# Two-layer attention and RWKV trunk: the next round's key norm begun in the levels, gates in the last round's levels, half the attention out projection in its chunk steps

## The chip, the cores and the metric

The kernel runs on one core of a Trainium2 chip. The metric is device time in microseconds (us), the median of its runs. PE is the matrix engine, DVE the vector engine, ACT the scalar (activation) engine, POOL the GpSimd engine, SP the engine that issues most DMAs; each runs its own instructions in the order in which they are written, and semaphores order the engines among one another.

## The reference

Two layers over 256 tokens of width 1024, float32. One layer, cut to what matters here:

```python
p = x @ w_in                                  # q, k, v, indexer; two gates; r, k, v, lora inputs of the RWKV part
y_a = dsa_sparse_mqa(...)                     # 8 heads over the top 64 keys that an indexer picks, then @ w_oa
kk = hd(k * k_k)
kk = kk / jnp.maximum(jnp.linalg.norm(kk, axis=-1, keepdims=True), 1e-12)      # the key norm
k = k * (1 + (a - 1) * k_a)
def step(state, inp):                         # 16 heads of 64, over 256 tokens
    sa = jnp.einsum('bhvk,bhk->bhv', state, -kk_t)
    state = state * w_t + sa[..., None] * b_t + v_t[..., None] * k_t
    return state, jnp.einsum('bhvk,bhk->bhv', state, r_t)
y_b = (group_norm(y) + bonus) * g @ w_ob
g_a, g_b = jnp.split(jax.nn.sigmoid(p_gate + b_gate), 2, axis=-1)
x = layer_norm(alpha * x + (g_a * y_a + g_b * y_b) @ w_out)
x = layer_norm(alpha * x + conv_glu_ffn(x))
```

## The kernel before

**A layer.** It runs through these stages: a prologue (projections, the indexer's scores), four rounds g = 0 to 3, the attention out projection ("oa", four pairs of weight slots), the RWKV one ("ob", four pairs), the mix ("out") and the feed-forward network ("up", "down"). Weights come through a ring of four slots that SP fills in the order of stream_order.

**A round.** It handles 4 of the 16 heads. The recurrence is done in 4 chunks of 64 tokens. PE first makes the grams (L836 and L877, which read arc, the scaled kk and r, and b_k, the scaled b and k) and turns v, b and k to token rows (V, tokB, tokK). Then come six levels of a doubling inverse on 64x64 blocks: per level W (copied out by ACT, L1246), X and Y (copied by DVE with a mask, L1572, and transposed, L1577), and W^T Y at the last. Then four chunk steps Z, Q, S, y, each a matmul, an ACT or DVE step, and the next matmul. All this is small and serial, so PE is given other products in between: fill(n) is called at 14 gaps of the levels and 8 of the chunk steps, and runs what the tables put there. A *piece* is half of one weight slot's product: 12 matmuls of 128x256 (three rounded parts per product, L700 to L702) inside the rounds; ahead of the first round the pieces are plain float32 (L679), two to a slot.

**What the tables put where.** LEVEL_GAPS puts the 8 pieces of the next round's r and k projections (pairs "rkv") into the levels, chunk_pairs its v projection and one gate (two in the last round) into the chunk steps. The last round has nothing in its levels. Five further gaps hold fixed work: the attention's logits, y_back (the last round's y turned back), the bonus, the probabilities' transposes (L818) and the values (L828 to L830). A slot's weights are split on ACT and DVE: "mid" (cast L1143, remainder L1462, two buffers) for pieces in rounds, "split" (cast L1178, remainder L1697, four buffers) for whole pairs after them.

**The preparation of a round.** It makes arc and b_k from the r and k projections. In the rounds before it: prep_kk on ACT (squares of the scaled key, L1190) after att_o; prep_1 on PE (decay and a lora products, L743 and L746) after the levels; then ACT's tanh (L1197), DVE's prep_decay (L1490 to L1494) and ACT's exponentials; prep_2 (in layer 1 the value lora's product; the key's sums of squares "ss", L764, 8 matmuls) after chunk 0, prep_3 (rnT, L769) after chunk 1, prep_4 (rnx, L778) after chunk 2; DVE's prep_sum, prep_rn and prep_rest (kkn L1533 to b_k L1551) in chunk steps 1 to 3. At a layer's start the same parts stand between the pieces of the first three gates, and DVE's two top-k searches (L1867 to L1880) stand between prep_sum, prep_rn and prep_rest. The grams wait for b_k and, after a round, for the sum of its y (y_sum, L1632).

**After the rounds.** PE does pairs oa 0 and 1, y_back, oa 2 and 3, ob 0 to 3. DVE centres, scales and gates y (L1632 to L1657), the halves yb 0 and yb 1 are rounded for ob, and gated_o (L1946) takes an oa pair's sum out of PSUM.

## Time and profile before

| what | value |
|---|---|
| runs | 1255.3, 1255.31, 1260.0 us |
| median | 1255.31 us |
| the profiled execution: its own time | 1254.65 us |
| its span, first to last instruction | 1252.4 us |
| mean granted PE clock | 0.977 |
| PE busy | 1152.6 us (92%) |
| DVE busy | 785.4 us (63%) |
| ACT busy | 539.0 us (43%) |
| POOL busy | 54.5 us (4%) |

Times in the rows below are us from the start of the span. A granted clock of 1.00 is 2.4 GHz, 0.50 is 1.2 GHz. Busy says how long an engine had an instruction in it, the brackets of a timeline row how long it stood idle before it and what released it.

### The profile page before, as it was taken

To read this page: it belongs to the slowest core of one execution; us is meant where nothing else is said; L and a number is where in the kernel's file an instruction comes from. 1 tells how busy PE (TensorE), PEld (TensorE's weight loads), DVE (VectorE), ACT (ScalarE), POOL (GpSimd) and SP (SyncE) were. 2 spreads that over 40 slices of the span, in tenths; PEclk is the share of its full clock that TensorE was granted. 3 is DMA by queue.
4 is the path that set the end of the run, shared out by engine and by line. 5 is a ranking of instruction groups with operands and counts; after the bars stand their busy time and mean duration, and the time that the engine had idled before them with its cause. 6 is when DMAs were issued, how large, how long until landed. Compare 5 with 4: busy or idle time off the path is not lost.

```text
span 1252.4 us, 29267 instructions
## 1 busy us (share of the span) xinstructions
PE 1152.6 (92%) x12328; PEld 1038.1 (83%) x12328; DVE 785.4 (63%) x1436; ACT 539.0 (43%) x938; POOL 54.5 (4%) x56
## 2 busy tenths in 40 slices
PE   7997998997899899999899979989978998999997
PEld 7777887876789799998797768878767897999985
DVE  1267576667476777774512775757584767777745
ACT  2243535353354355553212445353534443555531
POOL 0000000000000100000100000000000001000000
PEclk9999999999999899999999999999999998999998
DMA  7422221211175456556454221212111754555561
GB/s 283 147 90 77 85 91 50 83 52 61 35 260 178 162 178 195 182 195 200 152 179 147 77 73 69 94 53 87 42 53 38 265 170 168 179 192 178 193 200 69
DMA packets 45353, 165.38 MB, mean 132 GB/s; under 512 B 5136, under 2 KB 5392, under 8 KB 44976
## 3 DMA queue, kind: packets, MB, share of 16 engines
q1 hardware_dynamic: 42576, 154.02, 36.6%
q0 software_dynamic: 1504, 7.47, 1.8%
q8 instruction: 98, 1.61, 0.5%
q10 hardware_dynamic: 1152, 2.10, 0.5%
q14 instruction: 23, 0.19, 0.0%
HBM read 160.42 MB, written 3.15 MB: 131 GB/s over the span
## 4 chain that ended last, share of the span: by engine, by line
PE 76%; DVE 16%; issue 3%; ACT 3%; DMA 1%; DVEq 0%; SPq 0%; ACTq 0%
PE ps L700 18%; PE ps L701 16%; PE ps L702 16%; PE ps L836 8%; PE ps L679 5%; PE ps L986 3%; DVE ring_r L1462 2%; PE ps L848 1%; DVE keep L1873 1%; PE ps L1028 1%; DVE small L1871 1%; DMA ring<-stream_dram 1%; DVE X_Y L1577 1%; DVE X_Y L1572 1%; DVE keep L1860 1%
## 5 line engine op out<-in xcount | busy, mean ns | idle before, releaser
L700 PE MATMUL ps<-x_tok_r,mid_hi 128*128 128x256 f32 x448 | 137.7, 307 | 13.7 <-DVE ring_r L1462 12.5
L701 PE MATMUL ps<-xT_r,mid_hi 128*128 128x256 f32 x448 | 127.1, 284 | 0.0
L702 PE MATMUL ps<-x_tok_r,ring_r 128*128 128x256 f32 x448 | 126.9, 283 | 0.0
L700 PEld LDWEIGHTS ps<-x_tok_r,mid_hi 128*128 128x128 f32 x448 | 85.8, 191 | 23.4 <-issue 15.6
L679 PE MATMUL ps<-xT,ring 128*128 128x256 f32 x448 | 99.7, 381 | 0.0
L679 PEld LDWEIGHTS ps<-xT,ring 128*128 128x128 f32 x448 | 84.2, 190 | 13.0 <-issue 1.6
L701 PEld LDWEIGHTS ps<-xT_r,mid_hi 128*128 128x128 f32 x448 | 86.1, 192 | 0.0
L702 PEld LDWEIGHTS ps<-x_tok_r,ring_r 128*128 128x128 f32 x448 | 86.0, 192 | 0.0
L1572 DVE COPY_PREDICATED X_Y<-masks,ps 128x256 f32<-128x256 uint32 x80 | 35.1, 439 | 63.1 <-PE ps L836 55.3
L1462 DVE TENSOR_TENSOR ring_r<-ring,mid_hi 128x1024 fp32r<-128x1024 f32 x56 | 68.0, 1218 | 5.2 <-ACT mid_hi L1143 4.7
L1697 DVE TENSOR_TENSOR w_lo<-ring,w_hi 128x1024 fp32r<-128x1024 f32 x44 | 53.9, 1225 | 26.6 <-ACT w_hi L1178 26.5
L1697 DVE TENSOR_TENSOR rs_ks_r<-ring,tha_kkn_r 128x1024 fp32r<-128x1024 f32 x46 | 56.3, 1225 | 21.4 <-ACT tha_kkn_r L1178 21.4
L1697 DVE TENSOR_TENSOR vs_dC_r<-ring,b_k_r 128x1024 fp32r<-128x1024 f32 x46 | 56.1, 1220 | 17.4 <-ACT b_k_r L1178 17.4
L1697 DVE TENSOR_TENSOR X_Y_r<-ring,arc_r 128x1024 fp32r<-128x1024 f32 x44 | 53.7, 1222 | 21.1 <-ACT arc_r L1178 21.1
L1178 ACT CAST tha_kkn_r<-ring 128x1024 fp32r<-128x1024 f32 x46 | 47.9, 1041 | 33.7 <-PE ps L702 33.7
L1143 ACT CAST mid_hi<-ring 128x1024 fp32r<-128x1024 f32 x56 | 58.7, 1052 | 8.2 <-PE ps L702 8.2
L836 PE MATMUL ps<-X_Y,nT_rb 64*64 64x64 f32 x1280 | 54.2, 225 | 8.2 <-DVE ak_rk L1564 3.1
L1246 ACT COPY W_bt<-ps 128x256 f32<-128x256 f32 x80 | 29.5, 372 | 71.3 <-PE ps L836 51.1
L701 PE MATMUL ps<-oT_r,tha_kkn_r 128*128 128x256 f32 x208 | 59.8, 288 | 0.0
L836 PEld LDWEIGHTS ps<-X_Y,nT_rb 64*64 64x64 f32 x1280 | 44.6, 137 | 17.0 <-DVE X_Y L1572 7.4
L701 PE MATMUL ps<-oT_r,w_hi 128*128 128x256 f32 x208 | 58.4, 281 | 0.0
L701 PE MATMUL ps<-oT_r,arc_r 128*128 128x256 f32 x208 | 58.4, 281 | 0.0
(435 smaller groups left out, 3385.1 us busy)
## 6 DMA issues: line engine op xcount, KB each, us to landing
ring<-stream_dram SPq DMA_DIRECT2D x281, 512.0 KB, 3.5
lora_w<-lora_dram POOLq DMA_DIRECT2D x2, 1536.0 KB, 7.4
W_bt<-rpar_dram POOLq DMA_DIRECT2D x4, 512.0 KB, 5.2
kt_V<-rpar_dram POOLq DMA_DIRECT2D x4, 512.0 KB, 6.0
x_tok<-x_dram SPq DMA_DIRECT2D x2, 512.0 KB, 4.1
v_saved_dram<-vs_dC ACTq DMA_DIRECT2D x4, 256.0 KB, 4.0
x_tok<-x_dram SPq DMA_DIRECT2D x1, 1024.0 KB, 4.8
vf<-v_saved_dram ACTq DMA_DIRECT2D x4, 256.0 KB, 3.9
```

The costliest lines, as they stand in the source:

```text
L679: mm = pe.matmul(dst[:, b, :], w[:, kb * P:kb * P + P], rhs[:, kb, :], start=(kb == 0), stop=(kb == KB - 1))
L700: pe.matmul(dst, lh, rh, start=start, stop=False)
L701: pe.matmul(dst, lh, rl, start=False, stop=False)
L702: return pe.matmul(dst, ll, rh, start=False, stop=stop)
L836: mm = pe.matmul(dst[q], left[q, u, :], right[q], start=start, stop=stop)
L986: mm = pe.matmul(dst, xT[:, kb, t * P:t * P + P], w[:, kb * P:kb * P + n], start=(kb == 0), stop=(kb == KB - 1))
L1143: act.copy(mid_hi[m % NM][:, :], ring[:, n % RING, :]).then_inc(*act_mid.inc(l, m))
L1178: act.copy(w_hi[m % NS], ring[:, n % RING, :]).then_inc(*act_split.inc(l, m))
L1246: act.copy(W[:, 4 * k:4 * k + 4, :], half64("W", k)).then_inc(*act_wkv.inc(r, f"W{lev}{k}"))
L1462: dve.tensor_tensor(rounded["ring"][:, k, :], ring[:, k, :], f32(mid_hi[m % NM][:, :]), ALU.subtract).then_inc(*dve_mid.inc(l, m))
L1572: dve.copy_predicated(dst[:, 4 * k:4 * k + 4, :], mask_of(which, lev, 4), half64("XW", k)).then_inc(*dve_wkv.inc(r, name))
L1697: dve.tensor_tensor(w_lo[m % NS], ring[:, n % RING, :], f32(w_hi[m % NS]), ALU.subtract).then_inc(*dve_split.inc(l, m))
```

## The change

In words, by place:

- **Levels, g = 1 to 3:** LEVEL_GAPS becomes gaps 0, 1 and 4 to 9 (it was 0 to 7). tokK, which stood alone between gaps 1 and 2, is interleaved with W of level 1; its akV, rkV and ktV move half a level on each.
- **The last round:** its two gates (8 pieces) go into the levels, the pairs oa 0 and 1 (8 pieces, now "mid") into the chunk steps. After the rounds stand oa 2 and 3 alone, y_back after three of their four blocks; ob starts on yb 0 and waits for yb 1 at its seventh block of rows.
- **The next round's preparation:** ss moves from chunk 0 to gap 13 of the levels, rnT from chunk 1 to chunk 0, rnx from chunk 2 to chunk 1; prep_kk on ACT from after att_o to ahead of att_pT in level 4. DVE's prep_rest is cut into keys (c = 1), arc (c = 2) and v, b, k (c = 3).
- **A layer's start:** the parts between the pieces are now (ss), (lora products), (value lora), (rnT); rnx comes after the eighth piece; DVE takes ss first, ahead of prep_decay.

```diff
-LEVEL_GAPS = [list(range(4, 12))] + [list(range(8))] * (GROUPS - 2)
+LEVEL_GAPS = [list(range(4, 12))] + [[0, 1] + list(range(4, 10))] * (GROUPS - 1)
+OA_EARLY = 2
...
 def chunk_pairs(g):
 
+    if g + 1 == GROUPS:
+        return [("oa", i) for i in range(OA_EARLY)]
+    return [("rkv", 3 * (g + 1) + 2)] + gates_of(g)
+
+
+def gates_of(g):
+
     start = GATES_FIRST + sum(GATES_CHUNKS[:g])
-    v = [("rkv", 3 * (g + 1) + 2)] if g + 1 < GROUPS else []
-    return v + [("gate", i) for i in range(start, start + GATES_CHUNKS[g])]
+    return [("gate", i) for i in range(start, start + GATES_CHUNKS[g])]
+
+
+def level_pairs(g):
+
+    return [("rkv", 3 * (g + 1)), ("rkv", 3 * (g + 1) + 1)] if g + 1 < GROUPS else gates_of(g)
...
+            def prep_ss(r):
+
+                l, g = divmod(r, GROUPS)
+                if g == 0:
+                    pe.wait_ge(*act_att(l, "qT"))
+                else:
+                    pe.wait_ge(*act_wkv(r - 1, "ktV"))
                 pe.wait_ge(*act_prep(r, "kk2"))
                 for b in range(GB):
                     for t in range(TT):
                         j = 2 * (TT * b + t)
-                        mm = pe.matmul(bank(7)[:, j:j + 2], tmp[:, b, t * P:t * P + P], C["hsel"], start=True, stop=True)
+                        mm = pe.matmul(bank(4)[:, j:j + 2], tmp[:, b, t * P:t * P + P], C["hsel"], start=True, stop=True)
                 mm.then_inc(*pe_prep.inc(r, "ss"))
 
-            def prep_3(r):
+            def prep_rnT(r):
...
                         w = per_head(half64("W", k)[:, u - 4 * k, :], nT, X[:, u, :], u)
                         if u == 4 * k + 3:
                             w.then_inc(*pe_wkv.inc(r, f"W1{k}"))
-                        side = swapped(unit64(5)[:, u, :], ak[:, u, :], Vc[:, u, :])
+                        if u == 0:
+                            pe.wait_ge(*dve_wkv(r, "akrk"))
+                        side = turned_unit(unit64(5), k_of, u, OTHER)
                     if k == 0:
                         fill(4)
...
+                    if g + 1 < GROUPS and c == 1:
+                        prep_rnx(r + 1)
                     if c:
                         pe.wait_ge(*dve_wkv(r, f"Z{c}"))
                     for b, u in enumerate(bc(c)):
                         mm = per_head(step64(3)[:, b, :], Y, Zs[:, b, :] if c else akV[:, u, :], u)
                     mm.then_inc(*pe_wkv.inc(r, f"Q{c}"))
                     fill(15 + 2 * c)
+                    if g + 1 < GROUPS and c == 0:
+                        prep_v(r + 1)
+                        prep_rnT(r + 1)
...
                 first = sum([pair_pieces(l, ("gate", i), xT) for i in range(GATES_FIRST)], [])
-                for k, p in enumerate((prep_1, prep_2, prep_3, prep_4)):
+                for k, p in enumerate((prep_ss, prep_1, prep_v, prep_rnT)):
                     p(r0)
                     for piece in first[2 * k:2 * k + 2]:
                         piece()
+                prep_rnx(r0)
                 for piece in first[8:]:
                     piece()
...
-                        more = pair_pieces(l, ("rkv", 3 * (g + 1)), xT) + pair_pieces(l, ("rkv", 3 * (g + 1) + 1), xT)
-                        for n, p in enumerate(more):
-                            gaps[LEVEL_GAPS[g][n]].append(p)
+                    for n, p in enumerate(sum([pair_pieces(l, p, xT) for p in level_pairs(g)], [])):
+                        gaps[LEVEL_GAPS[g][n]].append(p)
...
+                    if g + 1 < GROUPS:
+                        gaps[VALUES].append(lambda: prep_ss(r0 + g + 1))
...
-                pe.wait_ge(*dve_parts(l, "o1"))
-                split_pair(l, ("oa", 0), lambda kb: (block_of(o_hi, kb), rounded["oT"][:, kb, :]))
-                split_pair(l, ("oa", 1), lambda kb: (block_of(o_hi, kb), rounded["oT"][:, kb, :]))
+                oa = [b for i in range(OA_EARLY, 4) for b in split_blocks(l, ("oa", i), o_parts)]
+                for block in oa[:-1]:
+                    block()
                 y_back(r0 + GROUPS - 1)
-                for i in (2, 3):
-                    split_pair(l, ("oa", i), lambda kb: (block_of(o_hi, kb), rounded["oT"][:, kb, :]))
-                pe.wait_ge(*dve_parts(l, "yb1"))
+                oa[-1]()
+
+                def yb_parts(kb):
+                    if kb in (0, 6):
+                        pe.wait_ge(*dve_parts(l, f"yb{kb // 6}"))
+                    return block_of(yb_hi, kb), rounded["yb"][:, kb, :]
+
                 for i in range(4):
-                    split_pair(l, ("ob", i), lambda kb: (block_of(yb_hi, kb), rounded["yb"][:, kb, :]))
+                    for block in split_blocks(l, ("ob", i), yb_parts):
+                        block()
 
...
                         for t in range(2):
-                            if nxt and level_before(g, t) == lev:
-                                rkv(l, g + 1, t)
+                            if level_before(g, t) == lev:
+                                if nxt:
+                                    rkv(l, g + 1, t)
+                                else:
+                                    gate(l, gates_of(g)[t][1])
                         if lev == 4:
+                            if nxt:
+                                prep_kk(r + 1)
                             att_pT(l, g)
+                        if not nxt and lev == 4:
+                            act.copy(o_hi[0], blocks(oT, 0, 4)).then_inc(*act_parts.inc(l, "o0"))
                     att_o(l, g)
+                    if not nxt:
+                        act.wait_ge(*act_att(l, f"o{g}"))
+                        act.copy(o_hi[1], blocks(oT, 4, 4)).then_inc(*act_parts.inc(l, "o1"))
...
+
+                prep_ss(r0)
                 prep_decay(r0)
-                prep_sum(r0)
+                prep_pend(r0)
                 topk(0)
                 prep_rn(r0)
                 topk(1)
-                prep_rest(r0)
+                prep_keys(r0)
+                prep_arc(r0)
+                prep_v(r0)
+                prep_bk(r0)
                 prep_bonus(r0)
...
                                 rkv(l, g + 1, t)
                         if lev == 3:
                             att_norm(l, g)
+                        if not nxt and lev == 4:
+                            o_low(0)
                     if nxt:
...
                         prep_decay(r + 1)
+                    if not nxt:
+                        o_low(1)
...
-                                                  f32(o_hi[c - 2]), ALU.subtract).then_inc(*dve_parts.inc(l, f"o{c - 2}"))
+                            if nxt and c == 1:
+                                prep_keys(r + 1)
+                            elif nxt and c == 2:
+                                prep_arc(r + 1)
+                            elif nxt:
+                                prep_v(r + 1)
+                                prep_bk(r + 1)
                         if c < NCH - 1:
                             chunk_s(r, c)
+                        if nxt and c == 0:
+                            prep_pend(r + 1)
+                            prep_rn(r + 1)
```

PE at the first layer's start. The rows follow the indexer's last score; lora,lora_w are the lora products of prep_1, const,tmp is ss (two units in a row), xT,ring the float32 pieces of gate 0. Of before:

```order
L743 MATMUL ps<-lora,lora_w 128x256 [waits act_att,lora_landed,act_lora]
L746 MATMUL ps<-lora,lora_w 128x256
L743 MATMUL ps<-lora,lora_w 128x256
L746 MATMUL ps<-lora,lora_w 128x256
L679 MATMUL ps<-xT,ring 128x256 [waits slot0_landed,dve_dense]
L679 MATMUL ps<-xT,ring 128x256 x3
L679 MATMUL ps<-xT,ring 128x256 [waits slot0_landed]
L679 MATMUL ps<-xT,ring 128x256 x3
L764 MATMUL ps<-const,tmp 128x2 [waits act_prep]
L764 MATMUL ps<-const,tmp 128x2 x3
```

Of the change:

```order
L798 MATMUL ps<-const,tmp 128x2 [waits act_prep,act_att]
L798 MATMUL ps<-const,tmp 128x2 x3
L697 MATMUL ps<-xT,ring 128x256 [waits slot0_landed,dve_dense]
L697 MATMUL ps<-xT,ring 128x256 x3
L697 MATMUL ps<-xT,ring 128x256 [waits slot0_landed]
L697 MATMUL ps<-xT,ring 128x256 x3
L770 MATMUL ps<-lora,lora_w 128x256 [waits act_att,lora_landed,act_lora]
L773 MATMUL ps<-lora,lora_w 128x256
L770 MATMUL ps<-lora,lora_w 128x256
L773 MATMUL ps<-lora,lora_w 128x256
```

The sums of squares stand ahead of the lora products, and a whole slot of gate 0 (16 matmuls) stands between the two.

ACT in levels 4 and 5 of the first round. rs_ks<-ps takes out the next round's k projection, scratch<-ps is att_pT, W_bt<-ps the copies of W for level 5, mid_hi the cast of a weight slot, oT the values, tmp<-rs_ks prep_kk. Of before:

```order
L1132 ACTIVATE rs_ks<-ps,dpar 128x256 [waits slot_used]
L1132 ACTIVATE rs_ks<-ps,dpar 128x256
L1237 COPY scratch<-ps 128x768 [waits pe_att]
L1246 COPY W_bt<-ps 128x256 [waits pe_wkv]
L1143 CAST mid_hi1<-ring 128x1024 [waits slot_used,slot3_landed]
L1246 COPY W_bt<-ps 128x256 [waits pe_wkv]
L1241 COPY oT<-ps 128x512 [waits pe_att]
L1190 ACTIVATE tmp<-rs_ks,cpar 128x256 [waits pe_bonus,dve_dense]
L1190 ACTIVATE tmp<-rs_ks,cpar 128x256
```

Of the change:

```order
L1181 ACTIVATE rs_ks<-ps,dpar 128x256 [waits slot_used]
L1181 ACTIVATE rs_ks<-ps,dpar 128x256
L1239 ACTIVATE tmp<-rs_ks,cpar 128x256 [waits pe_bonus,dve_dense]
L1239 ACTIVATE tmp<-rs_ks,cpar 128x256
L1286 COPY scratch<-ps 128x768 [waits pe_att]
L1295 COPY W_bt<-ps 128x256 [waits pe_wkv]
L1192 CAST mid_hi1<-ring 128x1024 [waits slot_used,slot3_landed]
L1295 COPY W_bt<-ps 128x256 [waits pe_wkv]
L1290 COPY oT<-ps 128x512 [waits pe_att]
```

prep_kk has moved ahead of att_pT and of both copies of W, and it waits for DVE's side of the k projection (dve_dense).

DVE at the end of the last round. b_k and ring_r are splits of weights (here named by the buffers they share), gates<-gates is gated_o, yt<-ps the sum of y, g8, yt and yb its norm. Of the change:

```order
L1673 TENSOR_TENSOR Zs<-ps,sq 128x128 [waits pe_wkv]
L1758 TENSOR_TENSOR w_lo2<-ring,w_hi2 128x1024 [waits act_split]
L1693 TENSOR_TENSOR yt<-ps,yt 128x512 [waits pe_wkv,act_wkv]
L1953 SCALAR_TENSOR_TENSOR gates<-gates,ps 128x512 [waits act_dense,slot_used]
L1697 TENSOR_REDUCE g8<-yt 128x8 [waits dve_y]
L1699 TENSOR_SCALAR g8<-g8 128x8 [waits dve_y]
L1701 TENSOR_TENSOR yt<-yt,g8 128x512 [waits dve_y]
L1758 TENSOR_TENSOR X_Y_r<-ring,arc0_r 128x1024 [waits act_split]
L1706 TENSOR_REDUCE g8<-sq 128x8 [waits act_y]
L1710 TENSOR_TENSOR yt<-yt,g8 128x512 [waits pool_y]
L2027 TENSOR_TENSOR yb_r<-yb,yb_hi0 128x1024 [waits act_parts]
L2027 TENSOR_TENSOR yb_r<-yb,yb_hi1 128x512
```

Of before, from the sum of y on (L1697 is a split there, and L1636 the reduction that is L1697 above):

```order
L1632 TENSOR_TENSOR yt<-ps,yt 128x512 [waits pe_wkv,act_wkv]
L1636 TENSOR_REDUCE g8<-yt 128x8 [waits dve_y]
L1638 TENSOR_SCALAR g8<-g8 128x8 [waits dve_y]
L1640 TENSOR_TENSOR yt<-yt,g8 128x512 [waits dve_y]
L1645 TENSOR_REDUCE g8<-sq 128x8 [waits act_y]
L1697 TENSOR_TENSOR X_Y_r<-ring,arc0_r 128x1024 [waits act_split]
L1649 TENSOR_TENSOR yt<-yt,g8 128x512 [waits pool_y]
L1697 TENSOR_TENSOR rs_ks_r<-ring,tha_kkn_r 128x1024 [waits act_split]
L1946 SCALAR_TENSOR_TENSOR gates<-gates,ps 128x512 [waits act_dense,slot_used]
```

The sum of y and the norm behind it stand among fewer splits, and with one gated_o ahead of the centring.

## Rows read from the trace of the kernel before

**Rows 1.** The page, part 4: the chain that ended last, share of the span by engine.

```profile
PE 76%; DVE 16%; issue 3%; ACT 3%; DMA 1%; DVEq 0%; SPq 0%; ACTq 0%
```

**Rows 2.** Waits of PE, whole span: line, tile, releaser, us in total, times, longest us.

```profile
PE ps L836 <- DVE yt L1632: 15.0, 6, 2.5
...
PE ps L818 <- DVE scratch L1686: 6.2, 6, 1.0
PE ps L836 <- DVE b_k L1551: 6.1, 2, 4.1
```

**Rows 3.** Windows: stretch, us; busy us and instructions of each engine; granted clock, DMA.

```profile
296.94:329.07 32.13, 25.84 (x632) 22.17 (x633) 20.63 (x42) 11.78 (x30) 1.83 (x2) 0.89 0.04 13
329.07:351.43 22.36, 18.92 (x232) 16.73 (x233) 9.64 (x17) 8.06 (x14) 0.00 (x0) 1.00 0.22 72
351.43:363.10 11.67, 11.67 (x102) 11.53 (x100) 8.53 (x11) 7.27 (x9) 2.94 (x4) 1.00 0.91 337
168.81:206.50 37.69, 34.85 (x729) 31.28 (x729) 26.72 (x50) 17.06 (x39) 2.80 (x2) 1.00 0.21 68
```

**Rows 4.** Windows of round starts and of one idle stretch, columns as in rows 3.

```profile
168.81:171.65 2.84, 2.83 (x128) 2.77 (x128) 1.45 (x4) 0.00 (x0) 0.00 (x0) 1.00 0.34 128
232.05:236.61 4.56, 4.56 (x129) 4.49 (x129) 1.61 (x4) 0.00 (x0) 0.00 (x0) 0.63 0.19 74
421.40:427.00 5.60, 1.51 (x10) 0.85 (x8) 4.94 (x8) 2.29 (x3) 1.56 (x1) 0.98 0.00 0
426.80:433.60 6.80, 6.05 (x27) 5.68 (x28) 6.80 (x10) 3.86 (x5) 1.10 (x2) 0.50 0.52 207
```

**Rows 5.** Timeline, first layer's start: start, us, engine, line, op, tiles, count.

```profile
77.88 0.90 ACT L1190 ACTIVATE tmp<-rs_ks,cpar 128x256 f32<-128x256 f32 x2
...
78.27 3.72 PE L679 MATMUL ps<-xT,ring 128*128 128x256 f32 x16
78.68 0.82 ACT L1197 ACTIVATE dA<-ps,dpar 128x256 f32<-128x256 f32 x2
...
81.83 0.95 PE L764 MATMUL ps<-const,tmp 128*128 128x2 f32 x8
...
82.90 0.28 DVE L1867 TENSOR_TENSOR keep<-keep,const 128x128 f32<-128x128 f32 x1
```

**Rows 6.** Timeline, level 4 of the first round: ACT and DVE.

```profile
138.87 0.80 ACT L1237 COPY scratch<-ps 128x768 f32<-128x768 f32 x1
...
139.88 0.37 ACT L1246 COPY W_bt<-ps 128x256 f32<-128x256 f32 x1 [0.21 <-PE ps L836]
...
140.26 0.83 DVE L1453 SCALAR_TENSOR_TENSOR rs_ks<-ps,cpar,rs_ks 128x255 f32<-128x255 f32 x2
...
143.12 0.91 ACT L1190 ACTIVATE tmp<-rs_ks,cpar 128x256 f32<-128x256 f32 x2
```

**Rows 7.** Timeline, end of the second round, start of the third: DVE, then PE.

```profile
230.09 1.22 DVE L1462 TENSOR_TENSOR ring_r<-ring,mid_hi 128x1024 fp32r<-128x1024 f32 x1
...
231.22 0.68 DVE L1632 TENSOR_TENSOR yt<-ps,yt 128x512 f32<-128x512 f32 x1
...
232.05 0.33 PE L836 MATMUL ps<-arc,b_k 64*64 64x128 f32 x2 [2.50 <-DVE yt L1632]
```

**Rows 8.** Waits of PE in the last round of the first layer.

```profile
PE ps L848 <- DVE yt L1649: 1.9, 1, 1.9
PE ps L700 <- DVE ring_r L1462: 1.5, 2, 0.8
PE ps L836 <- DVE S L1625: 1.2, 3, 0.6
...
PE ps L836 <- DVE Zs L1612: 0.8, 1, 0.8
```

**Rows 9.** Timeline after the last round: DVE's sum of y, PE's first ob product.

```profile
353.88 0.68 DVE L1632 TENSOR_TENSOR yt<-ps,yt 128x512 f32<-128x512 f32 x1
...
370.87 0.39 PE L700 MATMUL ps<-o_hi,w_hi 128*128 128x256 f32 x1 [0.84 <-DVE gates L1946]
```

More of the change, by code:

```diff
@@ L100, in mid_gaps @@
     for g in range(GROUPS):
-        if g + 1 < GROUPS:
-            last += [GAPS * g + n for n in LEVEL_GAPS[g][1::2]]
+        last += [GAPS * g + n for n in LEVEL_GAPS[g][1::2]]
         last += [GAPS * g + 14 + chunk_gap(g, 2 * i + 1) for i in range(2 * len(chunk_pairs(g)))]
@@ L151 @@
 SPLIT = ("oa", "ob", "out", "up", "down")
-SPLITS = [s for s in SLOTS if s[1] in SPLIT]
+SPLITS = [s for s in SLOTS if s[1] in SPLIT and not (s[1] == "oa" and s[2] < 2 * OA_EARLY)]
 SPLIT_AT = {s: m for m, s in enumerate(SPLITS)}
 NS = 4
-MIDS = [s for s in SLOTS if s[1] == "gate" and s[2] >= 2 * GATES_FIRST or s[1] == "rkv" and s[2] % KB >= GB]
+MIDS = [s for s in SLOTS if s[1] == "gate" and s[2] >= 2 * GATES_FIRST or s[1] == "rkv" and s[2] % KB >= GB
+        or s[1] == "oa" and s[2] < 2 * OA_EARLY]
 MID_AT = {s: m for m, s in enumerate(MIDS)}
@@ L489, in trunk @@
         pool_att = by_layer("pool_att", ["eps", "rs"])
-        pe_prep = Steps(sem("pe_prep"), [["zw", "za"] + (["zv"] if r >= GROUPS else []) + ["ss", "rnT", "rnx"]
+        pe_prep = Steps(sem("pe_prep"), [["ss", "zw", "za"] + (["zv"] if r >= GROUPS else []) + ["rnT", "rnx"]
                                          for r in range(R)])
@@ L804, in att_logits @@
                 r = GROUPS * l + g
[L805 removed]
+                pe.wait_ge(*act_wkv(r, "tokB"))
                 for h in range(2):
@@ L1248, in levels @@
                 if lev == 1:
+                    act.wait_ge(*pe_wkv(r, "tokK"))
+                    act.copy(kt, unit64(5)).then_inc(*act_wkv.inc(r, "tokK"))
                     act.wait_ge(*pe_wkv(r, "akV"))
@@ L1392, in _ @@
                                 gate(l, i)
-                            else:
+                            elif kind == "rkv":
                                 rkv(l, g + 1, 2)
                         if c == 1 and nxt and l:
-                            prep_tanh(r + 1, "thv", "hv0", kkn, 6)
-                        if not nxt and c in (1, 2):
-                            act.wait_ge(*act_att(l, f"o{g}"))
-                            act.copy(o_hi[c - 1], blocks(oT, 4 * (c - 1), 4)).then_inc(*act_parts.inc(l, f"o{c - 1}"))
+                            prep_tanh(r + 1, "thv", "hv0", thv, 6)
                         if not nxt and c >= 2:
@@ L1881, in topk, with o_low, gated_o @@
                                       ).then_inc(*dve_att.inc(l, f"keep{t}"))
+                def o_low(i):
+                    dve.wait_ge(*act_parts(l, f"o{i}"))
+                    dve.tensor_tensor(blocks(rounded["oT"], 4 * i, 4), blocks(oT, 4 * i, 4), f32(o_hi[i]), ALU.subtract
+                                      ).then_inc(*dve_parts.inc(l, f"o{i}"))
+                def gated_o(i):
+                    dve.wait_ge(*pair_done(l, ("oa", i)))
+                    dve.wait_ge(*act_dense(l, ("gate", 7)))
+                    dst = flat2(gates[:, 2 * i:2 * i + 2, :])
+                    dve.scalar_tensor_tensor(out=dst, in0=dst, scalar=1.0, in1=bank(pair_at[l, ("oa", i)] % 2), op0=ALU.add,
+                                             op1=ALU.mult).then_inc(*dve_dense.inc(l, ("oa", i)))
+                prep_ss(r0)
                 prep_decay(r0)
-                prep_sum(r0)
+                prep_pend(r0)
                 topk(0)
```

171 lines of the change are left out of this document (87 added, 84 removed).

## Prediction, made before the changed kernel ran

> **What bounds the kernel now.** I read the chain that ended last first: PE 76%, DVE 16%, every other engine little [rows 1]. A change pays where it shortens PE's work or its waits, so PE's waits over the whole span came next. The largest inside the rounds is the grams' wait for the sum of y, 15.0 us in 6 round boundaries; 1.0 us six times ahead of the probabilities' transposes; and 6.1 in 2 at the first rounds' grams, of which the longest is 4.1, so 2.0 in one layer and 4.1 in the other [rows 2]. In those last two DVE is the bound: everything on DVE's chain from the decay to b_k sets the start of the rounds, and PE has time to spare. Then the windows by stage, for the round without pieces in its levels: of 32.13 us PE is busy 25.84, at a granted clock of 0.89; the chunk steps take 22.36, and the first half of the oa products after them 11.67 with no idle time [rows 3].
>
> PE's own work is the same in both kernels: pieces, sums and transposes are moved, none is added. So the sum is over waits, over cover for waits, and over the clock.
>
> **1. A layer's start.** Before, the lora products run under the end of the scores, and tanh starts at 78.68, while ACT ends prep_kk at 77.88 + 0.90 = 78.78 [rows 5]. Now ss comes first on PE and waits for prep_kk until 78.8, takes about 1.0 (the row of 0.95), then a whole slot of gate 0 runs, 3.56 (16 matmuls, 3.72 with the last one's end), then the lora products, 0.5 to their first half [rows 5]. So tanh starts at 78.8 + 1.0 + 3.6 + 0.5 = 83.9 instead of 78.7: 5.2 later. DVE's order is ss, decay, then both top-k searches, so the searches, which started at 82.90 without need of the decay [rows 5], queue behind it and start as much later. PE idles at the grams already, so nothing absorbs this: I take +5.2 in each layer, since the second runs the same steps in the same order. Bounds: 1.0 (ss alone, if a slot that lands late lets nothing in between) to 6.5. The Trainium skill ("TensorE: Matmul & The Clock Gate", architectural detail) says that ACT and DVE take their instructions strictly first in, first out, and that PE only pulls weight loads ahead. By that rule DVE cannot start a search ahead of the decay; the order rows and the rows of the start agree with it, since no search is seen ahead of pend.
>
> **2. The first round.** ACT's prep_kk now stands ahead of att_pT and of level 5's copies of W, and waits for DVE's part of the k projection, which ends at 140.26 + 0.83 = 141.1 [rows 6]. Then kk 0.91, att_pT 0.80: the first copy of W starts at 142.8 instead of 139.88 [rows 6], 2.9 later, and the last product of the inverse, both masks behind it and the chunk steps wait for it. Later rounds have that k projection done a level earlier, and don't meet this. Also +1.0 for ss in a gap where it stands alone, +0.1 for tokK, +1.0 in the chunk steps and -1.4 at the boundary (both under 3). Sum +3.7 in each layer. Bounds +1 (if the stall fills with pieces after all) to +4.5.
>
> **3. The second and third rounds, each.** Levels: pieces at gaps 4 to 9 cover the wait of 1.0 ahead of the probabilities' transposes [rows 2], with the starts on either side 1.25; against it ss +1.0, and one split of 1.22 [rows 7] that now stands ahead of a mask on DVE, half of it seen, +0.6. Chunk steps: they lose ss (-1.0), but rnT and rnx leave the places where they covered waits. The last round, which has none of them, shows what lies there: 1.2 for S in three, 0.8 for Zs, 1.5 for the split in two, 3.5 in all [rows 8]; I take 2.0 of it as coming back, so +1.0 net (bounds -1.0 to +2.5). Boundary: before, DVE does keys, arc and b_k in the last chunk step, then a split of 1.22 and the sum of y, and PE waits 2.50 [rows 7]. Now only b_k stands there; the split waits for its cast, and the sum of y ends about 1.4 earlier: -1.4 (bounds -2.2, all but the sum itself, and 0 where the value steps of the second layer take their place). Together +0.3 a round (1.0 - 1.25 + 0.6 + 1.0 - 1.4, and rounding up), +0.6 a layer.
>
> **4. The clock at round starts.** The third round's grams and token turns take 4.56 at a granted clock of 0.63, the second's 2.84 at 1.00 [rows 4]: a stretch at 1.2 GHz costs 1.7. The windows show it in one of these two rounds in the first layer and in both in the second, each time right behind the boundary wait. With the wait halved I take them as gone: -1.7 and -3.4. Bounds 0 to that.
>
> **5. The last round.** With 8 pieces in its levels it is as long as a round that has them: the second round takes 37.69 to its chunk steps at full clock [rows 3], less the lora products of a next round (1.1), and little else: 36.7 against 32.13, +4.6. This holds the loss of its stretches at half clock, 0.89 over 32.13 [rows 3], and waits that the pieces now cover, y_back's 1.9 above all [rows 8]. The chunk steps keep 8 pieces, now oa's instead of gates, and stay at 22.4. After them oa 0 and 1 are gone: -11.7 [rows 3]. Less 0.2 for ACT's cast of o that now delays a copy of W. Sum -6.9 in each layer. Bounds -4.5 (no clock regained, oa's pieces wait for the attention's parts) to -8.
>
> **6. Behind the last round.** What hid y's norm is halved. From the sum of y at 353.88 to ob's first product at 370.87 are 17.0 us, at whose end PE waits 0.84, 1.0 from start to start [rows 9]. Now the sum of y can start at once, and fewer splits lie in the chain: 16.5. PE has until then four blocks of oa, 11.7, y_back 1.1, and ob up to its seventh row block, 6/8 of 2.9, 2.2: 15.0. So 1.5 to 1.8 at that wait, 0.8 for the gated_o that frees a bank, 0.25 for y_back: 2.8 in place of 1.0, +1.8 in each layer. Bounds 0 to +4.
>
> **Sum.** First layer 5.2 + 3.7 + 0.6 - 1.7 - 6.9 + 1.8 = +2.7; second 5.2 + 3.7 + 0.6 - 3.4 - 6.9 + 1.8 = +1.0; +3.7. Last, the clock where idle time is added: at 421.40 a stretch of 5.60 with 1.51 busy is followed by 6.80 at 0.50 [rows 4]. PE's idle time at the first rounds' grams grows from 2.0 and 4.1 to 7 and 8, and the grams and turns behind it or the levels after them, would then cost 1.7 more once or twice: I take +2.3, between one and two. That gives +6.0 on 1254.65, the profiled execution's own time (span 1252.4 and 2.25 around it, 0.7 under the median): 1260.65, rounded to 1260.5. The Trainium skill (same page, "Why this matters for your kernels") asks for no long idle gaps between bursts of matmuls; by it alone both layer starts would lose their clock. The trace agrees at 426.80.
>
> **The rivals.**
> - *Slower by over 0.5%: the clock.* The long idle stretches at both layer starts and the 2.9 in the first round each draw a stretch at 1.2 GHz (4 of 1.7), and those at the boundaries stay (5.1), since PE still waits there. 3.7 + 6.8 + 5.1 is +15.6, 1270.3; with half of these +9.6, 1264.3, so about 1266 as its middle. From two stretches more than I count it is over the bound. For it: three of four later rounds show such stretches after waits of only 2.5. Against it: the first rounds' waits of 2.0 and 4.1 show a stretch each already, so longer ones need not draw more.
> - *Faster by over 0.5%.* The start costs only what ss costs, 1.0 a layer, since DVE's and ACT's later work closes up (then -8.4), and the copy of W waits for nothing (-5.8, since pieces in gap 12 cover it). The other terms stand: 3.7 - 8.4 - 5.8 is -10.5, 1244. For it: PE and DVE both have slack around the searches. Against it: DVE is busy through nearly all of that stretch, and PE waits for it at its end.
> - *No change at all:* the last round's pieces move the waits behind the round, +5 there instead of +1.8, while step 1 is half as large: about 1255 to 1258. It lies on the forecast's side of the bound.
>
> **How the numbers follow.** The kernel's runs and this working can tell 0.5% (6.3 us) from no change; so faster is under 1249.0, slower over 1261.6. The likeliest case, a loss at the layer starts and in the first round that outweighs the gain of the last rounds by little, with the rival of no change beside it: 0.47. Over 0.5% slower, the clock rival and the upper part of the bounds of steps 1, 2 and 6: 0.39. Faster, 0.14. The range of 1249 to 1268 leaves out the faster case but for its edge, and the far end of the clock's.
>
> **What would show it.** In the changed kernel's trace: the first top-k search and the first grams start about 5 us later in each layer (first layer: grams near 109); PE waits about 3 us for ACT's copy of W in level 5 of the first round, and not in the others; the boundary waits are near 1.1 instead of 2.5 and the round behind them starts at a clock of 1.00; the last round takes 36 to 38 us to its chunk steps; from there to ob about 15 us, with a wait of 1.5 for yb 1. The prediction is wrong if the searches start where they did, if the boundaries keep their 2.5, or if the mean granted clock moves by more than 0.01.

## The result and the profile after

The changed kernel takes 1274.71 us in the median (1271.55 to 1279.1, four runs) against 1255.83 for the kernel before beside it: a ratio of 1.0145, with a 95% interval of 1.0104 to 1.0187. In a second set of runs it was 1273.36 against 1256.07, a ratio of 1.0151 (1.0125 to 1.0177). The forecast was 1260.5 with a range up to 1268, so it missed by 14 us. The way was right, the size was not. The mean granted clock went from 0.977 to 0.964, which the prediction had named as a sign that it is wrong (a move of more than 0.01).

The waits of PE over the whole span, in the changed kernel, columns as in [rows 2]:

```profile
PE ps L722 <- DVE ring_r L1516: 16.4, 21, 2.3
PE ps L869 <- DVE b_k L1612: 12.8, 2, 7.3
...
PE ps L869 <- DVE S L1686: 9.9, 24, 0.6
PE ps L851 <- DVE scratch L1747: 9.3, 6, 1.8
PE ps L869 <- ACT W_bt L1295: 7.8, 8, 2.4
...
PE ps L869 <- DVE yt L1693: 6.2, 6, 1.0
PE ps L798 <- ACT tmp L1239: 3.3, 2, 1.6
...
PE ps L869 <- DVE nT_rb L1625: 3.0, 2, 1.5
```

The boundary wait for the sum of y fell from 15.0 to 6.2, and the longest from 2.5 to 1.0, as forecast. The wait for b_k at the first rounds rose from 6.1 to 12.8. Those for ACT's copy of W rose from 3.6 to 7.8, the longest from 0.8 to 2.4. New are the waits for the squares of the key and, once in each first round, 1.5 for DVE's masked grams (the row of nT_rb). Before, PE turned k to token rows inside that wait, so that it was two, of 0.7 and 1.1. The one ahead of the probabilities' transposes, which step 3 had as covered, rose from 6.2 to 9.3.

Windows by stage of the changed kernel, PE alone (stretch, length, busy us and instructions, granted clock, DMA): the start of the first layer from the last score to the grams, its three rounds, the last round's levels, its chunk steps, what lies behind them to ob, and the second layer's start and first round.

```profile
78.50:114.49 35.99, 28.33 (x126) 0.87 0.29 95
114.49:187.32 72.83, 61.94 (x956) 0.88 0.17 53
187.32:249.73 62.41, 55.85 (x987) 1.00 0.23 74
249.73:316.43 66.70, 60.33 (x987) 0.92 0.22 69
316.43:352.97 36.54, 33.95 (x729) 1.00 0.32 108
352.97:375.50 22.53, 19.12 (x234) 1.00 0.22 71
375.50:390.10 14.60, 12.65 (x128) 1.00 0.79 262
711.10:745.85 34.75, 25.76 (x129) 0.96 0.29 92
745.85:819.59 73.74, 62.85 (x959) 0.88 0.17 56
```

Between the same instructions in both kernels, with the time at 1.2 GHz (a granted clock of 0.50) in brackets, summed from the trace's clock records. "First round" and the like are the rounds g = 0, 1 and 2:

| stage, us (of these at 1.2 GHz) | before | changed | difference | my step |
|---|---|---|---|---|
| layer 1: scores to grams | 26.86 (0) | 35.99 (9.6) | +9.1 | +5.2 |
| first round | 65.07 (3.4) | 72.83 (17.7) | +7.8 | +3.7 |
| second | 63.23 (0) | 62.42 (0) | -0.8 | +0.3 |
| third | 64.89 (3.4) | 66.70 (10.2) | +1.8 | +0.3 - 1.7 |
| last round to ob | 79.68 (6.8) | 73.67 (0) | -6.0 | -6.9 |
| ob to the next scores | 319.53 (13.7) | 321.00 (13.7) | +1.5 | +1.8 |
| layer 2: scores to grams | 29.78 (0) | 34.75 (2.7) | +5.0 | +5.2 |
| first round | 64.99 (3.4) | 73.74 (17.8) | +8.8 | +3.7 |
| second and third | 131.39 (7.4) | 130.22 (6.8) | -1.2 | +0.6 - 3.4 |
| last round to ob | 79.61 (6.3) | 72.34 (0) | -7.3 | -6.9 |
| ob to the end | 250.43 (13.1) | 252.58 (12.7) | +2.2 | +1.8 |

"Layer 1" and "layer 2" are the first and second layer. The first stage, up to the scores, is 1.6 longer in the changed kernel's profile, which has nothing of the change in it; in the profiles of this case it lies anywhere from 76.3 to 79.3. Where the time at 1.2 GHz is about equal on both sides, the difference is within 1.6 of my step. Where it grew most (first rounds, first layer's start, third round), it is 3 to 5 us above it. In all the span holds 91.3 us at 1.2 GHz instead of 57.5.

The places themselves, in the timeline of the changed kernel. First the first layer's start:

```profile
79.48 0.90 ACT L1239 ACTIVATE tmp<-rs_ks,cpar 128x256 f32<-128x256 f32 x2
...
80.53 1.42 PE L798 MATMUL ps<-const,tmp 128*128 128x2 f32 x8 [1.65 <-ACT tmp L1239]
81.81 6.66 PE L697 MATMUL ps<-xT,ring 128*128 128x256 f32 x16
...
89.57 0.84 ACT L1246 ACTIVATE dA<-ps,dpar 128x256 f32<-128x256 f32 x2 [9.19 <-PE ps L773]
...
90.44 0.43 DVE L1544 TENSOR_SCALAR dA<-dA 128x512 f32<-128x512 f32 x1 [8.29 <-ACT dA L1246]
...
93.63 0.28 DVE L1928 TENSOR_TENSOR keep<-keep,const 128x128 f32<-128x128 f32 x1
...
114.47 0.48 PE L869 MATMUL ps<-arc,b_k 64*64 64x128 f32 x2 [5.48 <-DVE b_k L1612]
```

PE waits for the squares of the key, the lora products come after a slot of gate 0, and ACT's tanh starts 89.57 instead of 78.68 [rows 5], DVE's first top-k search 93.63 instead of 82.90. Of these 10.7 to 10.9 us, 1.6 are the later scores and 5.2 my step. The rest is mostly that slot running at half clock: it takes 6.66 here, and 3.70 in the same place of a kernel of experiment 5, whose clock is full there. Then level 5 of the first round, ACT and PE:

```profile
153.64 0.91 ACT L1239 ACTIVATE tmp<-rs_ks,cpar 128x256 f32<-128x256 f32 x2 [2.15 <-DVE rs_ks L1507]
154.45 0.78 ACT L1286 COPY scratch<-ps 128x768 f32<-128x768 f32 x1
155.13 0.37 ACT L1295 COPY W_bt<-ps 128x256 f32<-128x256 f32 x1
...
155.55 0.62 PE L869 MATMUL ps<-X_Y,W_bt 64*64 64x64 f32 x14 [2.45 <-ACT W_bt L1295]
```

ACT stands 2.15 us ahead of prep_kk, which waits for DVE's side of the k projection, and the copy of W queues behind it, where it stood free in [rows 6]. A window of what follows, on the same kernel:

```profile
156.10:162.90 6.80, 6.80 (x48) 0.50 0.00 0
```

PE is busy all through it, at 1.2 GHz.

### The profile page after: what moved, and what is told of

Same layout as the page of the kernel before. It is cut to its first block, busy times and chain, and to the rows that moved or that the text cites. A ratio compares the mean times of both kernels' runs of the same rounds, so it can differ in the third digit from the quotient of the medians.

```text
span 1274.8 us, 29251 instructions
## 1 busy us (share of the span) xinstructions
PE 1160.5 (91%) x12328; PEld 1042.2 (82%) x12328; DVE 785.9 (62%) x1436; ACT 537.2 (42%) x938; POOL 50.6 (4%) x56
## 4 chain that ended last, share of the span: by engine, by line
PE 76%; DVE 17%; ACT 3%; issue 3%; DMA 1%; POOL 0%; DVEq 0%; SPq 0%; ACTq 0%
PE ps L722 18%; PE ps L723 16%; PE ps L724 16%; PE ps L869 8%; PE ps L697 5%; PE ps L1028 3%; DVE ring_r L1516 3%; DVE keep L1934 1%; PE ps L1070 1%; PE ps L881 1%; DVE small L1932 1%; PE ps L798 1%; PE ps L770 1%; ACT mid_hi L1192 1%; DMA ring<-stream_dram 1%
## 5 line engine op out<-in xcount | busy, mean ns | idle before, releaser
L697 PE MATMUL ps<-xT,ring 128*128 128x256 f32 x448 | 102.8, 388 | 0.0
L1516 DVE TENSOR_TENSOR ring_r<-ring,mid_hi 128x1024 fp32r<-128x1024 f32 x64 | 77.9, 1219 | 25.0 <-ACT mid_hi L1192 25.0
L1192 ACT CAST mid_hi<-ring 128x1024 fp32r<-128x1024 f32 x64 | 67.2, 1054 | 12.7 <-PE ps L724 12.7
L1227 ACT CAST arc_r<-ring 128x1024 fp32r<-128x1024 f32 x42 | 43.7, 1040 | 29.0 <-PE ps L724 19.3
L723 PE MATMUL ps<-oT_r,tha_kkn_r 128*128 128x256 f32 x192 | 55.7, 290 | 0.0
L1227 ACT CAST b_k_r<-ring 128x1024 fp32r<-128x1024 f32 x44 | 45.8, 1040 | 19.9 <-PE ps L724 19.9
L723 PE MATMUL ps<-oT_r,b_k_r 128*128 128x256 f32 x192 | 53.9, 281 | 0.0
```

The costliest lines, as they stand in the source:

```text
L697: mm = pe.matmul(dst[:, b, :], w[:, kb * P:kb * P + P], rhs[:, kb, :], start=(kb == 0), stop=(kb == KB - 1))
L723: pe.matmul(dst, lh, rl, start=False, stop=False)
L1192: act.copy(mid_hi[m % NM][:, :], ring[:, n % RING, :]).then_inc(*act_mid.inc(l, m))
L1227: act.copy(w_hi[m % NS], ring[:, n % RING, :]).then_inc(*act_split.inc(l, m))
L1516: dve.tensor_tensor(rounded["ring"][:, k, :], ring[:, k, :], f32(mid_hi[m % NM][:, :]), ALU.subtract).then_inc(*dve_mid.inc(l, m))
```

## Experiments

They ran in three sets, each on a chip of its own and beside the kernel before, whose median was 1256.21 in the first (start_old, kk_late, both_old, last_only), 1256.07 in the second (after_again, warm_waits, prep_fixed, best_warm) and 1256.89 in the third (warm_waits2, best_warm2, ss_then_lora, prep_fixed2). The changed kernel ran in its own set (1274.71) and in the second (1273.36), so most differences from it go across sets; by the kernel before, such a difference is good to about 1 us. Ratios are to the kernel before of the same set, and stage times are those of one profiled execution each.

**1. The order at a layer's start put back.**

```diff
-                for k, p in enumerate((prep_ss, prep_1, prep_v, prep_rnT)):
+                for k, p in enumerate((prep_1, prep_v_ss, prep_rnT, prep_rnx)):      # prep_v_ss: prep_v, then prep_ss
...
-                prep_ss(r0)
                 prep_decay(r0)
                 prep_pend(r0)
+                prep_ss(r0)
```

> The change with the order at a layer's start put back on PE and DVE (lora products and decay first, the sums of squares after the first slot of gate 0), all else as changed. Theory 1 (waits alone): the stages from the scores to the first grams go back from 35.99 and 34.75 us to about 27 and 30, so 13 us come back and nothing else moves: about 1262. Theory 2 (waits and the clock they draw): the stretches at 1.2 GHz ahead of the grams go as well and with them those of the first rounds' levels, 2 to 4 us more: 1257 to 1260. Rival (the start is hidden by what follows): 1270 or more.

1255.24 us, ratio 0.9988 (0.9966 to 1.001): 18 to 19 us less than the changed kernel, more than either theory said. Windows of this kernel, start and first round of the first and the second layer:

```profile
78.46:105.32 26.86, 24.73 (x126) 1.00 0.34 111
105.32:176.73 71.41, 59.88 (x956) 0.90 0.18 62
696.20:725.98 29.78, 25.59 (x129) 1.00 0.32 108
725.98:799.33 73.35, 62.23 (x959) 0.88 0.17 56
```

Both starts are to 0.01 us what they were before, and the time at 1.2 GHz in the first is gone. The first rounds are still long: they are the second experiment's.

**2. ACT's squares of the key behind the copies of W, in the first rounds.**

```diff
                         if lev == 4:
-                            if nxt:
+                            if nxt and g:
                                 prep_kk(r + 1)
                             att_pT(l, g)
...
+                    if g == 0:
+                        prep_kk(r + 1)
                     att_o(l, g)
```

In these rounds PE's sums of squares stand behind the attention's values.

> The change with, in the first round of each layer alone, ACT's squares of the key behind the copies of W of level 5 and the sums of squares behind the attention's values. Theory 1 (waits alone): PE's gap of 2.66 us ahead of the last product goes to under 0.5 in both layers, and 1.0 of work stands in the open: 3 to 4 us less, about 1271. Theory 2 (with the clock): the 6.8 us at 1.2 GHz that follow that gap go too, 3.4 each: 7 to 10 us less, about 1266. Rival (another wait ends there anyway, DVE's): less than 1.5 us.

1261.34 us, ratio 1.0025 (0.9999 to 1.0051): 12 to 13 less, more than either theory said. The profiled execution is the slowest of its ten (1266.99). Windows of the two first rounds:

```profile
114.70:181.67 66.97, 58.49 (x955) 0.92 0.18 59
...
742.99:810.69 67.70, 59.12 (x960) 0.92 0.19 61
```

They are 5.9 and 6.0 shorter, where the wait had been 2.45 (the 2.66 of the expectation stands in no row), and have 7 us less at 1.2 GHz. So a wait of 2.45 cost over twice itself. Ten runs of this kernel spread from 1252.91 (mean granted clock 0.979) to 1266.99 (0.968), and the time follows the clock with a correlation of -0.94: in this kernel the spread between runs goes with the clock.

**3. Both.**

> Both edits of the two kernels ahead of this one. Theory 1: the sum of waits, 1274.7 - 13 - 4 = about 1258. Theory 2: with the clock, 1250 to 1254. If the sum is far from the two single effects, the clock's stretches are drawn by both places together.

1245.6 us, ratio 0.9904 (0.9872 to 0.9935). From 1273.36 that is 28 less, near the sum of 18 and 12 of the single edits, so the two places act apart from one another. The rest of the change makes the kernel 1% faster. Even here the first rounds hold 6.8 and 10.2 us at 1.2 GHz, where the kernel before has 3.4 each: the wait for the masked grams stays in them, now 1.75 long:

```profile
PE ps L870 <- DVE nT_rb L1633: 1.8, 1, 1.8
```

Behind it stands a wait of 2.74 for a weight split, which the kernel before has too (2.73). What the first of the two costs was not tried alone.

**4. The last round's part alone.** The kernel before, with gates_of, level_pairs, OA_EARLY, the new gaps for the last round alone, the split of o in level 4 and the shorter tail from the diff above, and nothing of the preparation.

> The kernel before with the last round's part alone (its gates in the levels, oa 0 and 1 in the chunk steps, oa 2 and 3 behind), the preparation and the other rounds as before. My step 5 and 6 give 5.1 us less in each layer: about 1245. The stages of the changed kernel from the last round's grams to the mix show 6.0 less in the first layer with 1.4 given back at ob: 1246. Rival (what is gained in the last round is given back behind it, by the wait for yb 1 and the clock): 1253 to 1257.

1252.3 us, ratio 0.9954 (0.9934 to 0.9974). In the profile the stretch from the last round's grams to ob is 75.8 instead of 79.7 in the first layer and 74.3 instead of 79.6 in the second, 9.2 less together, near my 10.2 for steps 5 and 6. By the medians only 3.9 are gained, and the time is next to the rival's 1253 to 1257. In that profile 1.7 us are given back ahead of the first scores and 1.4 in the two first rounds, which the edit doesn't touch, and its execution was one of the faster (1248.43, at a clock of 0.979). What else separates 9.2 from 3.9 isn't settled.

**5. The same waits, with PE kept busy in them.** The changed kernel ran again, in the second set.

> The changed kernel itself, beside the others of this set on one chip: about 1274 again.

1273.36 us (1269.74 to 1277.53). In the others, matmuls of constants, written where nobody reads, stand ahead of three of PE's waits in each layer: for the squares of the key, for the first grams and for the copy of W. All other work is the changed kernel's. The diff is that of the second such kernel.

```diff
+            def warm(n, b):
+                for _ in range(n):
+                    pe.matmul(tok(b)[:, 0, :], C["bones"], C["scan"][:, 0:T], start=True, stop=True)
...
+                if g == 0:
+                    pe.wait_ge(*act_att(l, "s5"))
+                    warm((12, 15)[l], 2)
                 pe.wait_ge(*dve_prep(r, "bneg"))
...
+                    warm(4, 5)
                 pe.wait_ge(*act_prep(r, "kk2"))
...
+                        if g == 0 and lev == 5 and k == 0:
+                            pe.wait_ge(*act_wkv(r, "rkV"))
+                            warm(5, 5)
                         pe.wait_ge(*act_wkv(r, f"W{lev}{k}"))
```

A first kernel had too many of them, behind the wait ahead of the grams.

> The change with all its waits, and matmuls of constants that nobody reads (0.22 us each) put into four of PE's waits in each layer: 9 ahead of the wait for the squares of the key at the layer's start, 24 and 30 ahead of the first grams, 10 ahead of the wait for the copy of W in level 5 of the first round. Theory 1 (waits alone): the waits are as long as they were, 1274 stays to 2 us. Theory 2 (the clock): the stretches at 1.2 GHz in the stages from the scores to the second round's grams (27.3 and 20.5 us of them in the changed kernel) fall to under half, and the time falls by 8 to 14 us, to 1260 to 1266. If the clock falls although PE is kept busy, what draws it is something else.

1291.51 us, ratio 1.0286, and no test: the two starts were 45.9 and 50.7 us long with the matmuls themselves in the way. It gave their price, 0.44 us, and its first rounds were 71.16 and 70.84 with 6.8 us at 1.2 GHz in each, instead of 72.83 and 73.74 with 17.7 and 17.8. Mended:

> As warm_waits, mended: one such matmul takes 0.44 us, not 0.22, and those ahead of the grams stood behind the wait that they were to fill. Now 4, 12 and 15, and 5 of them, ahead of the waits. Theory 1 (waits alone): 1273. Theory 2 (the clock): in the first warm_waits the first rounds had 9 and 11 us less at 1.2 GHz and were 1.0 and 3.0 us shorter in spite of 1.8 us of matmuls too many; so 3 to 5 us less in each first round, 1 to 3 at the first layer's start, in all 8 to 12: 1261 to 1265.

1258.15 us, ratio 1.0018 (0.9998 to 1.0039), where the changed kernel has 1273.36 and 1.0151 (another set). Windows, start and first round of both layers:

```profile
78.55:111.10 32.55, 31.72 (x157) 1.00 0.33 105
111.10:180.18 69.08, 59.83 (x965) 0.95 0.19 56
700.40:735.08 34.68, 33.82 (x167) 1.00 0.30 93
735.08:805.31 70.23, 61.41 (x969) 0.93 0.19 59
```

The waits of the other engines are as long as they were, and the matmuls of constants end before what PE waits for. Level 5 of the first round, ACT, then PE:

```profile
149.51 0.91 ACT L1248 ACTIVATE tmp<-rs_ks,cpar 128x256 f32<-128x256 f32 x2 [2.15 <-DVE rs_ks L1516]
150.32 0.78 ACT L1295 COPY scratch<-ps 128x768 f32<-128x768 f32 x1
151.00 0.37 ACT L1304 COPY W_bt<-ps 128x256 f32<-128x256 f32 x1
...
148.91 2.43 PE L746 MATMUL ps<-const 128*128 128x256 f32 x10
151.42 0.68 PE L874 MATMUL ps<-X_Y,W_bt 64*64 64x64 f32 x16
```

The starts take 32.55 and 34.68, so 5.7 and 4.9 more than before, at a clock of 1.00: that is my 5.2. The first rounds take 4.0 and 5.2 more than before, with 3.4 and 6.8 us more at 1.2 GHz in them. With 52.8 us at 1.2 GHz in the span instead of 91.3 the kernel is 15 us faster with the same waits, and no change but the filled waits stands between the two kernels: the cause is the clock. By the profiles, the four stages with the filled waits give 10.8 of the 17.6 us against the changed kernel's first profile, and 8.5 of 10.3 against its second; the rest lies in stages where the time at 1.2 GHz changes from one execution to the next. What the first rounds still have at 1.2 GHz begins behind the wait for the masked grams, which was not filled: 0.5 us behind it in the second layer, 3.3 in the first, there within the wait for the split.

**6. The lora products right behind the sums of squares.**

```diff
-                for k, p in enumerate((prep_ss, prep_1, prep_v, prep_rnT)):
+                for k, p in enumerate((prep_ss_1, prep_v, prep_rnT, prep_rnx)):     # prep_ss_1: prep_ss, then prep_1
```

> The change with the lora products at a layer's start right behind the sums of squares, ahead of any piece; all else as changed. If the slot of gate 0 that stands between them is what costs (3.6 of the 5.2 us of my step 1), the stages from the scores to the grams are 26.9 + 2 to 3 and 29.8 + 2 to 3, and the time 1258 to 1262. If the wait for the squares of the key is what costs (1.6 and 1.0 behind it), they stay near 32 and 34.

1261.44 us, ratio 1.005 (1.0022 to 1.0079). The two starts in its windows:

```profile
78.01:108.83 30.82, 28.04 (x126) 0.89 0.26 89
699.96:731.14 31.18, 25.65 (x129) 1.00 0.32 103
```

This is what was expected if the slot costs. The second start, at a clock of 1.00, is 3.6 shorter than the changed kernel's: the slot of gate 0. The 1.4 that stay over the kernel before are the sums and the wait ahead of them. In the first layer 6.8 us at 1.2 GHz still follow that wait, and it is 30.8.

**7. The preparation alone, both orders put back.** In the first of two kernels one copy on ACT reads a PSUM bank that the new order doesn't write, so part of y is missing from its result; the second reads the right one.

> The kernel before with the preparation alone moved, its gaps and tokK interleaved, but with the two orders put back that the first set tried; the last round as before. By my steps 3 and 4 each layer gains 1.1 (first) and 2.8 (second), and the first round loses 0.8: about 1254. By difference of the first set (1245.6 with the last round's part, and that part alone 3.9 less than before) it is 1249.5. Rival (the preparation's moves are worth nothing, and the gain of both together is the last round's): 1256.

> As prep_fixed, with one copy on ACT taken from the PSUM bank that the new order writes; the same work and waits, so the same 1252.7.

1252.7 and 1252.1 us, ratios 0.9975 (0.996 to 0.9991) and 0.9966 (0.9945 to 0.9986). They are 3.4 and 4.8 under the kernel before. With the 3.9 of the last round's part this adds up to 7 to 9 of the 11 us by which both together beat the kernel before.

**8. Both orders put back, and PE kept busy in waits that the kernel before has too:** ahead of the first grams and of the transposes behind three of the layer norms. The first had too many again.

> The change with both orders put back, and matmuls of constants in PE's waits ahead of the first grams (8 and 17) and ahead of the transposes of each layer norm (14, three places). Clock theory: of some 48 us at 1.2 GHz in 1247 (profile of the kernel without them) about half goes, 8 to 12 us: 1235 to 1238. Waits alone: 1245.6, as without them.

> As best_warm with half as many matmuls of constants (4 and 8 ahead of the grams' wait, 7 ahead of each layer norm's transposes), so that none outlasts its wait. The first one had 0 and 5.5 us at 1.2 GHz in the stages behind the rounds instead of 13.7 and 11.1, and they were 2.1 and 3.4 us shorter with 2.9 us of matmuls too many in each layer norm. So 8 to 12 us less than 1245.6: 1235 to 1238. Waits alone: 1245.

1250.55 us (ratio 0.9955) and 1242.51 us (ratio 0.9894, 0.9863 to 0.9924). The window from ob to the next layer's scores, of both_old and then of best_warm2:

```profile
371.16:692.78 321.62, 309.89 (x2031) 0.98 0.53 174
```

```profile
374.25:692.94 318.69, 312.33 (x2059) 1.00 0.55 176
```

The clock stays at 1.00 there and 2.9 us come back, of 13.7 at 1.2 GHz. The time is 3 us under both_old's, in another set, within what these runs can tell, and not the 8 to 12 that I expected: the whole span has 42.7 us at 1.2 GHz instead of 52.1, since a stretch of 10.2 appears in its second round. Both are about 1% faster than the kernel before, and 2 to 2.5% faster than the change as it was made.

## Why the prediction was wrong

The step that failed is the last term of the sum, the clock where idle time is added, put at +2.3. In the profile the starts and first rounds are 12.9 us above steps 1 and 2, and filling their waits gave back 15 us in the median. Step 4, the clock regained at the round starts, put at -5.1, failed too: it was not had at all. The steps on waits held in the main.

- **Step 1 (layer starts, +5.2 each).** Right: +5.7 and +4.9 at full clock, 3.6 of it the slot. The grams began at 114.47, where I had 109. Taking the order back gave 18 to 19 us, because the clock's loss went with it.
- **Step 2 (first rounds, +3.7 each).** Right in place, and for the stall in size: PE waited 2.45 where I had 2.9. With the waits kept busy the rounds are 3.3 and 2.7 longer than those of both_old, at equal time at 1.2 GHz. The rest of the step was too dear: against the kernel before they are 4.0 and 5.2 longer, of which, at half of the added 3.4 and 6.8 us at 1.2 GHz (my estimate), 1.7 and 3.4 are the clock. Its terms add up to 3.6, not 3.7. As changed the rounds were 7.8 and 8.8 longer, with 14 us more at 1.2 GHz in each.
- **Step 3 (+0.3 a round).** A little too dear: -0.8 in the second round. Its terms add up to -0.05, and the +0.3 is no rounding of that. The boundary wait went from 2.50 to 1.03 (forecast 1.1). The wait for the probabilities did not go, it rose from 1.0 to 1.8 in these rounds: in the third round DVE is busy without a gap from 277.17 on, with the bonus and its side of the k projection just ahead of the probabilities. And the chunk steps' waits for S appear 24 times instead of 6. PE's waits in the second round add up to 6.3 instead of 5.8, and it is shorter all the same, because PE's busy time for the same 985 instructions fell from 57.01 to 55.86. I had taken PE's own work as the same in both. The turn of k, which stood alone before (32 small products, 1.15 us) and now stands among those of W, is the likely source; it was not tried alone.
- **Step 4 (the stretches at round starts, -1.7 and -3.4).** Right at the place, wrong in the sum. The second and third rounds' grams and turns take 2.9 us each at a clock of 1.00 in the first layer, but 10.2 us at 1.2 GHz appear later in the third round, and 3.4 in each of the second layer's second and third. All three begin 0.2 to 1.8 us behind the wait of 1.8 ahead of the probabilities' transposes, the one that step 3 had as covered. So the stretches moved within the round: these four rounds have 17.0 us at 1.2 GHz instead of 10.8, and are together 0.2 us shorter where I had 3.9.
- **Step 5 (-6.9 each).** The levels took 36.54 (forecast 36.7), the chunk steps 22.53, and from the last grams to ob -6.0 and -7.3. Right.
- **Step 6 (+1.8 each).** Right in place: PE waits 1.45 for yb 1 inside ob. ob and what follows is +1.5 and +2.2. That the size came out is in part luck. The row of 370.87 in [rows 9] is a product of oa (its operand is o_hi), and ob begins at 376.63 there. And from the sum of y at 375.50 to yb 1 the changed kernel takes 18.4 us where I had 16.5, while PE has 17.0 until it waits, where I had 15.0: y_back waits 1.5, not 0.25. The two misses cancel.
- **The clock.** I priced its return at one or two stretches of 1.7, and gave the case of four and more, "slower by over 0.5%: the clock", the place of a rival at about 1266 (the middle of its two figures is 1267.3). It was the case that came, and it went past my upper end of 1268. The profile before had the sign: 6.80 us at 0.50 behind an idle stretch of 5.60 [rows 4], twice the length that I counted for a place. In the changed kernel stretches of 6.8 us begin at 81.0, 111.7, 122.0 and 156.1 in the first layer, and at 743.2, 753.4 and 787.6 in the second, up to 3.4 us lost for each. They begin 0.5 us behind the wait for the squares (1.65), inside the one for the grams (5.48), 1.1 behind the one for the masked grams (1.51) and 0.5 behind the one for the copy of W (2.45). The third of these was in no step of mine. The Trainium skill ("TensorE: Matmul & The Clock Gate", "Why this matters for your kernels") asks to avoid idle gaps between bursts of matmuls; the fifth experiment agrees, with 15 us for filling three waits in each layer. The wait of 2.45 is shorter than the gaps that the page warns of, and 6.8 us at 1.2 GHz stood behind it all the same.

The two steps of an unmeasured size, the clock's gain and its loss, had opposite signs, and I weighed the loss by what was likely per place. PE is busy 92% of the span, so a us at 1.2 GHz costs a good part of the half that it can cost: the same round (g = 1 and 2 of the first layer, in the changed kernel and in kk_late) takes 62.4 us with none, 63.6 with 3.4 and 66.7 with 10.2.

## What to carry to other kernels

Here a new wait of 2.45 us cost over twice its length, and a start that came 5.2 later nearly twice that. In a kernel that PE bounds, look at the granted clock behind each wait of the kind in the trace before: if one shows 6.8 us at half clock, count up to 3.4 and not 1.7. And when a wait is taken away at one place, look for the next wait in the same round: the stretch can come there instead. Before moving a small step ahead on an engine, look at what its operands wait for and at what is queued behind it: here eight tiny matmuls and two activations, moved ahead of work that a long chain needed, cost more than all the gaps that the change filled were worth. Independent moves are worth timing one at a time: without these two orders the same change is 1% faster than the kernel before.

## What the runs showed of the hardware

Matmuls that nobody needs, put into three waits of each layer, made the changed kernel 15 us faster (1258.15 against 1273.36). Where they outlasted the wait or stood behind it, they cost their own time, 0.44 us each (float32, 128x128 by 128x256): nine in place of four, and twenty-four that stood behind the wait for the grams, made a start 45.91 us long instead of 32.55. Runs of one kernel differ by their clock: 1252.91 at 0.979 and 1266.99 at 0.968, on one chip in one set. But for the one that each profile ends in, stretches at 1.2 GHz came in lengths of 3.4, 6.8 and 10.2 us. Those of 10.2 stand at three kinds of place: at the transposes behind the first layer's first norm (in five profiles), once in a first round behind the wait for the masked grams (warm_waits2), and in the second or third round of four profiles (of the changed kernel twice, of kk_late and best_warm2), each behind the wait of 1.8 ahead of the probabilities' transposes. In the changed kernel's profile that is this row, and a window 1.8 us later:

```profile
280.63 0.33 PE L851 MATMUL ps<-const,scratch 128*128 128x128 f32 x1 [1.81 <-DVE scratch L1747]
```

```profile
282.40:292.60 10.20, 10.20 (x91) 0.50 0.01 2
```

Other rounds have the same wait and no such stretch; why it comes in some executions and not in others is open.
